# The samples' context in four column groups of TensorE, and a sample's final scores on VectorE in two turns

## The reference: what is computed

```python
def one_seq(args):                       # once for each of 8 samples
    qn_i, qr_i, pages, rows_i = args
    past = cache[pages].reshape(-1, CACHE_ROW)          # 2048 x 320
    rows = jnp.concatenate([past, rows_i], 0)           # + the sample's own row
    lat_i, kr_i = rows[:, :KV_LORA_RANK], rows[:, KV_LORA_RANK:]
    kn_i = key_nope(lat_i, w_uk, g_kn_nope)             # per head, rms-normalised
    return mla_attend(qn_i, qr_i, kn_i, kr_i, lat_i, ...)

# in mla_attend: s = scores of 8 heads x 2049 rows
p = jax.nn.softmax(s, axis=-1)
ctx = jnp.einsum('bhqk,bkc->bqhc', p, lat)              # 8 heads x 256
```

## Time and profile before

| | us |
|---|---|
| median of 3 runs | 3432.31 |
| lowest, highest | 3425.12, 3432.45 |
| the profiled execution's own time | 3436.75 |
| its span, first to last instruction | 3434.9 |
| TensorE busy | 2767.9 (81%) |
| VectorE busy | 2275.0 (66%) |
| ScalarE busy | 1041.1 (30%) |
| GpSimd busy | 1223.9 (36%) |
| mean granted TensorE clock | 0.887 |
| moved by DMA | 1264.74 MB |

### The profile page before, as it was taken

One profiled execution on the slowest core, in us unless ns is written; L12 is line 12 of the kernel. 1 busy time (PEld: TensorE's weight loads), 2 busy tenths in 40 slices (PEclk: granted clock), 3 DMA queues, 4 the chain that ended last, 5 costly groups with the idle time before them and its releaser, 6 DMA issues.

```text
span 3434.9 us, 39503 instructions
## 1 busy us (share of the span) xinstructions
PE 2767.9 (81%) x11255; PEld 1236.3 (36%) x11255; DVE 2275.0 (66%) x6378; ACT 1041.1 (30%) x4438; POOL 1223.9 (36%) x1077
## 2 busy tenths in 40 slices
PE   7898889979989878989988779889875675566766
PEld 2355554424434333434433244344331231112321
DVE  2444568887777876768776676777766545565455
ACT  1222324424334423434434314434311111111111
POOL 0000014434333434434434434433344444543343
PEclk8989999979999989989989989999988777777777
DMA  8740069999999999999999999999999999999998
GB/s 337 276 177 35 14 252 410 400 365 405 364 379 411 414 373 413 413 388 418 409 393 409 400 392 409 415 403 417 392 410 413 408 421 408 422 394 378 419 420 352
DMA packets 201396, 1264.74 MB, mean 368 GB/s; under 512 B 23689, under 2 KB 44730, under 8 KB 61393
## 3 DMA queue, kind: packets, MB, share of 16 engines
q0 software_dynamic: 150784, 1091.03, 77.8%
q1 hardware_dynamic: 50393, 171.18, 13.0%
HBM read 1258.79 MB, written 3.79 MB: 368 GB/s over the span
## 4 chain that ended last, share of the span: by engine, by line
PE 44%; DMA 29%; DVE 13%; issue 7%; ACT 3%; POOL 3%; SPq 0%; DVEq 0%; POOLq 0%; ACTq 0%; PEldq 0%
PE bank L1149 15%; DMA ring<-in_uv,work 14%; PE bank L887 7%; DMA big<-in_uv,work 7%; DMA mod_mix<-in_uv,work 6%; PE bank L999 5%; DVE ring L2031 2%; PE bank L833 2%; PE bank L904 2%; PE bank L701 2%; ACT work L1478 1%; DMA ring<-in_w_ada 1%; POOL ring L1517 1%; PE bank L639 1%; PE bank L731 1%
## 5 line engine op out<-in xcount | busy, mean ns | idle before, releaser
L1149 PE MATMUL bank<-ring,work 128*64 128x512 f32 (+1 forms) x2080 | 900.8, 706 | 243.7 <-ACT work L1478 243.7
L1517 POOL DMA_INDIRECT ring<-in_uv,work x520 | 609.8, 1173 | 906.2 <-PE bank L1149 781.1
L2031 DVE CUSTOM_DVE_ANT_0 ring<-ring,mod_smp 128x1024 f32<-128x1024 f32 x512 | 622.2, 1223 | 270.3 <-DMA ring<-in_uv,work 262.9
L1466 ACT ACTIVATE work<-work 128x2 f32<-128x2 f32 x520 | 105.1, 202 | 1478.2 <-DVE work L2031 1477.9
L1517 POOL DMA_INDIRECT big<-in_uv,work x260 | 309.0, 1189 | 670.8 <-PE bank L1149 369.5
L887 PE MATMUL bank<-big 128*128 128x512 f32 x1024 | 513.9, 625 | 0.0
L1149 PE MATMUL bank<-big,work 128*64 128x512 f32 (+1 forms) x1040 | 311.1, 716 | 157.9 <-ACT work L1478 157.9
L1149 PEld LDWEIGHTS bank<-ring,work 128*64 128x64 f32 (+1 forms) x2080 | 210.1, 153 | 593.4 <-ACT work L1478 356.7
L2031 DVE CUSTOM_DVE_ANT_0 big<-big,mod_smp 128x1024 f32<-128x1024 f32 x256 | 309.7, 1223 | 138.4 <-DMA big<-in_uv,work 134.6
L1149 PE MATMUL bank<-work 128*64 128x512 f32 (+1 forms) x520 | 292.9, 691 | 107.9 <-ACT work L1478 107.9
L1478 ACT ACTIVATE work<-small,work 128x64 f32<-128x64 f32 (+1 forms) x1040 | 303.2, 339 | 144.8 <-DVE work L2041 138.4
(11 more groups left out here) (301 smaller groups left out, 3422.5 us busy)
## 6 DMA issues: line engine op xcount, KB each, us to landing
big<-in_wk SPq DMA_DIRECT2D x48, 1152.0 KB, 10.4
ring<-in_w_ada SPq DMA_DIRECT2D x64, 768.0 KB
work<-in_cache_mla SPq DMA_DIRECT2D x104, 160.0 KB, 7.2
ring<-in_uv,work POOLq DMA_INDIRECT x520, 12.3
big<-in_uv,work POOLq DMA_INDIRECT x260, 12.2
ring<-in_w_mla_out SPq DMA_DIRECT2D x1, 4096.0 KB, 14.1
big<-in_w_mla_out SPq DMA_DIRECT2D x4, 1024.0 KB, 11.5
mod_smp<-in_cache_mla SPq DMA_DIRECT2D x24, 160.0 KB, 10.9
```

Source lines behind the costliest of these rows:

```text
L1149: last = mm(out, diag[:, t % 2, j, 0:min(m, HALF)], s[:, D + half * 512:D + (half + 1) * 512], start=(k == 0 and (n < S0 or j == 0)), stop ...
L1466: act.activation(acts[:, t % 2 * GRP:(t % 2 + 1) * GRP], dots[:, t % 2 * GRP:(t % 2 + 1) * GRP], ACT.Gelu)\
L1517: pool.indirect_dma_start(slot[g % SLOTS], None, T["uv"].rearrange("l e d -> (l e) d"), bass.IndirectOffsetOnAxis(index[:, k * GRP + j:k * ...
L2031: dve.tensor_tensor_reduce(u, u, hb, 1.0, 0.0, ALU.mult, ALU.add, dots[:, at:at + 1]).then_inc(sem("dots_set"), 1)
```

## The change

`tail` is given 8 turns instead of 7. `final_scores` stops after two of the three Newton steps, and a new `final_scores_end` does the rest in the next turn; everything behind it moves by one turn, `load_pages` on SP too. `context` writes block g to the column group g modulo 4 (output rows 0, 32, 64, 96). The first four blocks take 32 columns of `ps_all` as weights, so that all 32 rows of a group are written, of which 8 count; the rest take 8 columns. The four partial sums are not added there: `contexts` copies all 128 rows, unscaled, and `context_cols` multiplies each half with two slices of `fold` (ones where row modulo 64 equals the column), which transposes and adds in one. The division by the sum of the numerators moves behind it, into `keep_context`, for which `context` now spreads the sums to all 128 rows.

With it `tail` is at turns 34, 81, 121, 172, 215, 259, 302 and 345, and the samples' first pages at 2, 46, 89, 129, 180, 223, 270 and 310. The last page of sample 5 moves from turn 252 to 257.

```diff
@@ -243,7 +243,8 @@
         krn = region(big, NPG * NH, 16384)
         krt = region(big, NPG * NH, 16384)
         sc_s = region(big, (NPG + 1) * NH, 16384).rearrange("p (g h) -> p g h", g=NPG + 1)
-        ps_s = region(big, (NPG + 1) * NH, 16384).rearrange("p (g h) -> p g h", g=NPG + 1)
+        ps_all = region(big, (NPG + 1) * NH, 16384)
+        ps_s = ps_all.rearrange("p (g h) -> p g h", g=NPG + 1)
         ctx_s = region(big, KLC * NH * NS, 16384).rearrange("p (c h s) -> p c h s", c=KLC, h=NH)
         oT_s = region(big, NH * NS, 16384)
         pages = region(big, NS * NPG, 16384)[0:1].bitcast(I32)
@@ -339,8 +340,8 @@
                 page_turn[t_] = (r_, g_)
                 t_ += 2
             tail[r_] = t_
-            t_ += 7
-        out_turn = max(tail[NS - 1] + 7, head_turn(3, PH - 1) + 1)
+            t_ += 8
+        out_turn = max(tail[NS - 1] + 8, head_turn(3, PH - 1) + 1)
         assert out_turn + 10 < smp_open[S0], out_turn
 
         page_at = {page_turn[k]: k for k in page_turn}
@@ -528,7 +529,7 @@
                                 sp.wait_ge(sem("mix_w_free"), 3)
                             load_head(layer_of(n), i, h)
                 for r in range(1, NS):
-                    if t == tail[r - 1] + 4:
+                    if t == tail[r - 1] + 5:
                         sp.wait_ge(sem("ctx_ps"), r)
                         load_pages(r)
                 if t == AHEAD:
@@ -898,17 +899,21 @@
 
             def context(r):
                 pe.wait_ge(sem("p_sum"), r + 1)
-                mm(pb[6][0:NH, 144:145], tiny[:, 24:24 + NH], ones[:, 0:1], start=True, stop=True)
+                mm(pb[6][:, 144:144 + NH], ones[:, :], tiny[:, 24:24 + NH], start=True, stop=True)
                 pe.wait_ge(sem(f"page_in{NPG // PGRP}"), 16 * (r + 1))
                 for g in range(NPG + 1):
-                    last = mm(pb[6][0:NH, 160:160 + KL], ps_s[:, g, :], cached[g][:, 0:KL] if g < NPG else cached_own, start=(g == 0), stop=(g == NPG))
+                    at, m = g % 4 * 32, 32 if g < 4 else NH
+                    last = mm(pb[6][at:at + m, 160:160 + KL], ps_all[:, g * NH:g * NH + m], cached[g][:, 0:KL] if g < NPG else cached_own,
+                              start=(g < 4), stop=(g > NPG - 4), skip_group_check=True)
                 last.then_inc(sem("ctx_ps"), 1)
 
             def context_cols(r):
                 pe.wait_ge(sem("ctx_norm"), r + 1)
                 pe.sem_inc(sem("wait_done"), 1)
                 for c in range(KLC):
-                    last = pe.transpose(pb[6][:, 432 + c * NH:432 + (c + 1) * NH], ctx_n[c][0:NH, :], ident[0:NH, 0:NH])
+                    for a in range(2):
+                        last = mm(pb[6][:, 432 + c * NH:432 + (c + 1) * NH], ctx_n[c], fold[:, a * 32:a * 32 + NH],
+                                  start=(a == 0), stop=(a == 1), skip_group_check=True)
                 last.then_inc(sem("ctx_cols"), 1)
 
             def sample_heads():
@@ -1103,13 +1108,13 @@
                 if t in page_turn:
                     project_page(*page_turn[t])
                 for r in range(NS):
-                    if t == tail[r] + 1:
+                    if t == tail[r] + 2:
                         spread_max(r)
-                    if t == tail[r] + 2:
+                    if t == tail[r] + 3:
                         spread_max2(r)
-                    if t == tail[r] + 4:
+                    if t == tail[r] + 5:
                         context(r)
-                    if t == tail[r] + 6:
+                    if t == tail[r] + 7:
                         context_cols(r)
                 if t == out_turn:
                     sample_heads()
@@ -1533,10 +1538,11 @@
             d(tt(cact[:, :, 0:NC], hbuf[:, 0, 0:DC * NC].rearrange("p (c n) -> p c n", c=DC),
                  hbuf[:, 1, 0:DC * NC].rearrange("p (c n) -> p c n", c=DC), ALU.mult), "c_act")
 
-            def inverse_root(y, v, t, link):
-
-                link(ts(y.bitcast(I32), v.bitcast(I32), -0.5, float(0x5F3759DF), ALU.mult, ALU.add))
-                for _ in range(3):
+            def inverse_root(y, v, t, link, steps=(0, 1, 2)):
+
+                for step_ in steps:
+                    if step_ == 0:
+                        link(ts(y.bitcast(I32), v.bitcast(I32), -0.5, float(0x5F3759DF), ALU.mult, ALU.add))
                     link(tt(t, y, y, ALU.mult))
                     link(stt(t, t, -0.5, v, ALU.mult, ALU.mult))
                     link(stt(y, t, 1.5, y, ALU.add, ALU.mult))
@@ -1867,7 +1873,12 @@
                     w.next("own_in", 16)
                 e, at = chain(r, 0)
                 e(ts(kss[:, :], kss[:, :], 1.0 / NOPE, EPS, ALU.mult, ALU.add))
-                inverse_root(krn[:, :], kss[:, :], krt[:, :], e)
+                inverse_root(krn[:, :], kss[:, :], krt[:, :], e, (0, 1))
+
+            def final_scores_end(r):
+
+                e, at = chain(r, 8)
+                inverse_root(krn[:, :], kss[:, :], krt[:, :], e, (2,))
                 both = pb[6][:, 0:256].rearrange("p (g a h) -> p g a h", g=NPG, a=2)
                 e(tt(sc_s[:, 0:NPG, :], both[:, :, 0, :], krn[:, :].rearrange("p (g h) -> p g h", g=NPG), ALU.mult))
                 e(tt(sc_s[:, 0:NPG, :], sc_s[:, 0:NPG, :], both[:, :, 1, :], ALU.add))
@@ -1892,16 +1903,16 @@
 
             def contexts(r):
                 dve.wait_ge(sem("ctx_ps"), r + 1)
-                dve.reciprocal(tiny[0:NH, 32:33], pb[6][0:NH, 144:145]).then_inc(sem("smp_tail"), 1)
-                dve.wait_ge(sem("smp_tail"), r * 2 + 2)
+                dve.reciprocal(tiny[:, 24:24 + NH], pb[6][:, 144:144 + NH]).then_inc(sem("smp_tail"), 1)
                 for c in range(KLC):
-                    last = ts(ctx_n[c][0:NH, :], pb[6][0:NH, 160 + c * P:160 + (c + 1) * P], tiny[0:NH, 32:33], None, ALU.mult)
+                    last = ts(ctx_n[c], pb[6][:, 160 + c * P:160 + (c + 1) * P], 1.0, None, ALU.mult)
                 last.then_inc(sem("ctx_norm"), 1)
 
             def keep_context(r):
                 dve.wait_ge(sem("ctx_cols"), r + 1)
-                ts(ctx_s[:, :, :, r:r + 1].rearrange("p c h s -> p c (h s)"), pb[6][:, 432:432 + 2 * NH].rearrange("p (c h) -> p c h", c=KLC),
-                   1.0, None, ALU.mult).then_inc(sem("ctx_ready"), 1)
+                dve.wait_ge(sem("smp_tail"), r * 2 + 2)
+                tt(ctx_s[:, :, :, r:r + 1].rearrange("p c h s -> p c (h s)"), pb[6][:, 432:432 + 2 * NH].rearrange("p (c h) -> p c h", c=KLC),
+                   tiny[:, 24:24 + NH].unsqueeze(1).to_broadcast([P, KLC, NH]), ALU.mult).then_inc(sem("ctx_ready"), 1)
 
             def add_sample():
                 dve.wait_ge(sem("smp_out_ps"), 5)
@@ -1995,14 +2006,16 @@
                     if t == tail[r]:
                         final_scores(r)
                     if t == tail[r] + 1:
+                        final_scores_end(r)
+                    if t == tail[r] + 2:
                         top(r)
-                    if t == tail[r] + 2:
+                    if t == tail[r] + 3:
                         shift(r)
-                    if t == tail[r] + 3:
+                    if t == tail[r] + 4:
                         sums(r)
-                    if t == tail[r] + 5:
+                    if t == tail[r] + 6:
                         contexts(r)
-                    if t == tail[r] + 6:
+                    if t == tail[r] + 7:
                         keep_context(r)
                 if t == out_turn + 9:
                     add_sample()
```

## The result

| | us |
|---|---|
| before, median of 5 runs | 3432.45 |
| changed, median of 5 runs | 3450.32 (3446.35 to 3458.30) |
| ratio, with its 95% interval | 1.0051 (1.0038 to 1.0064) |
| changed, measured once more, median of 11 runs | 3445.99, ratio 1.0030 (1.0018 to 1.0042) |
| profiled execution of the changed kernel | 3446.35, span 3444.5 |

The change makes the kernel slower, by 0.3 to 0.5%. The forecast was 3421 us, and the time lies outside its range as well.

The account below looks back on a forecast made before the run. The DMAs were taken to bound the kernel, so only their dry time could return: -9 us (context), -2 (final_scores split), 0 (longer tail), in all -11 from 3432.3 to 3421 us; likeliest 3415 to 3427, 8 in 10 3407 to 3438.

Parts of the forecast that it names:

- What bounds: In the stage of the turns the DMAs set the pace; an engine counts only where the DMAs run dry.
- dry time: A window's length times one less its DMA share; 9.1 us at the tails' starts, 11.7 us from context on.
- Part 1, size: Context in column groups on TensorE: 2.2 us instead of 7.5 per sample, 9 us of kernel time given back.
- Part 1, the page load: TensorE's wait for the next sample's pages: about 2 of 7.00 us remain; 1 to 2 us new for sample 2.
- Part 3, sample 5: Sample 5's tail moves into the pooling mixer's turns: 0, between a gain of 2.5 us and a loss of 4.7.
- Part 2: final_scores in two turns on VectorE: 2.25 us move one turn on, 2 us gained, between 0 and 4.5.
- first windows: Four turns from each sample's tail (final_scores); samples 0 and 7 were to keep a DMA share of 0.90 to 0.95.
- rival (b): Windows from context on: bytes are right, the DMA share hides thin queues; up to 26 us back, 3406 us, chance 0.10.
- (d): Slower: less dense TensorE work in the tail keeps its clock low; some +8 us, 3440 us, chance 0.12.
- the windows from context on: Four turns from each sample's context; the granted clock there was to stay above 0.9.
- 0.97 or more in all windows: Sign that the forecast holds: a DMA share of at least 0.97 in every window from context on.

Follow-up runs that it names:

- second profile: The changed kernel measured once more without an edit, and profiled again: 3445.99 us, ratio 1.0030 to the kernel before.
- the padded kernel: The changed kernel with 24 useless TensorE instructions behind the context, after the signal that releases the page loads: 3439.16 us, ratio 1.0016 to the kernel before.
- the groups alone: The kernel before with only the context in four column groups, tail of 7 turns and final_scores in one: 3428.13 us, ratio 0.9985.

## Why the prediction was wrong, point by point

- **What bounds.** Right in the main. The largest losses appear as dry time of the DMAs; the busy time of TensorE fell by 27.5 us and bought nothing by itself. But turns 270 to 302 are 4 to 5 us longer than before at a share of 1.01, which dry time doesn't explain and no run here does.
- **Part 1, size.** Right: 2.3 us for 2.2 forecast, full overlap. By itself it gained 5 us where 9 were taken.
- **Part 1, the page load: the first step that failed.** I had written that of the 7.00 us wait "about 2 us of that remain", and took 1 to 2 us for sample 2 (the prediction names a load by the sample whose tail it ends, so these are the pages of sample 3, in turn 128). Measured were 13.3 us in the one place (turn 222 now) and 10.6 in the other. I had moved the release 5.3 us forward and kept the time to landing as it was. But that time was short before because TensorE, 7.5 us in its context, freed no slots, and the gathers' queue ran down: to 0.4 to 1.3 MB at the first issue for samples 2, 3, 5 and 7, against 1.5 to 3.3 MB in the changed kernel. POOL in turn 86 of the kernel before:

```profile
1005.42 0.94 POOL L1517 DMA_INDIRECT work<-in_uv,work  x1 [10.38 <-PE bank L1149]
```

  The shorter context removed the pause in which the pages had the DMAs nearly to themselves. What TensorE's stand costs is seen best in turns 220 to 232, between kernels with the same turns: the changed kernel (a stand of 13.27 us, and 79.5 us of length in its second profile), and the padded one (1.80 us).

```profile
1751.12:1831.77 80.65, 64.96 (x286) 31.32 (x284) 47.66 (x149) 26.23 (x127) 29.56 (x26) 0.87 0.94 365
```

```profile
1749.97:1824.07 74.10, 66.51 (x304) 31.70 (x303) 48.20 (x149) 26.27 (x126) 27.97 (x24) 0.95 1.01 403
```

  That is 5 to 7 us for this one stand, although the padded kernel has 5.34 us more work in these turns. Behind samples 1 and 6, with stands as long, the same comparison gives 1 us or nothing (turns 81 to 95: 86.9 and 85.8; 302 to 317: 84.5 and 85.2).

- **Part 3, sample 5: the second step that failed, and the larger one.** I had the move in the right place, and set it to 0 between a gain of 2.5 and a loss of 4.7 us, from VectorE's busy time alone. Measured: turns 254 to 270 went from 103.1 to 110.7 us (106.7 in the second profile), and dry time between turns 257 and 267 from 4.1 to 17.4 us (13.0). The 32 turns behind add 4 to 5 us. VectorE's busy time in turns 254 to 270 is the same before and after (79.7 and 79.6 us), so a sum of busy times could not show this; what I had left out is how a tail's steps and the mixer's hold each other up when they share turns. One part of it is seen: VectorE's stand for `spread_max` behind 7.5 us of matmuls, 6.68 us where it was 4.50. Taking that wait away gave nothing that can be measured. How the rest divides between the tail's steps and the page that now lies in these turns stays open.
- **Part 2.** Right in the main: nothing to gain where VectorE is full. The first windows of samples 0 and 7 went from 0.83 and 0.91 to 0.86 and 0.93. In sample 5's crowded turns the split did help, which I hadn't said; the time shows it clearly only against the second measurement of the changed kernel.
- **Rivals.** The slower side was named, 12%, but with the wrong mechanism. (The sum of rival (b) is short of its own words: 26 us and part 2's 4.5 give 3402, not 3406.) The clock did fall in the windows from context on (0.76 and 0.76 for samples 1 and 2, from 1.00 and 0.99), as (d) said. But TensorE stands for pages in just these windows, so the clock is as much a result as a cause. With the groups alone, where the stand in turn 87 is 2.0 us, turns 86 to 90 have a clock of 0.93, and that kernel is faster. Two windows, those of samples 1 and 2 (here from tail + 5 to tail + 9, in answer to the earlier trace rows):

```profile
990.54:1025.85 35.31, 21.93 (x129) 10.84 (x127) 19.80 (x63) 9.04 (x30) 9.02 (x9) 0.76 0.99 372
1225.60:1253.90 28.30, 16.57 (x77) 6.96 (x71) 15.99 (x33) 5.67 (x24) 7.45 (x7) 0.76 1.02 405
```

  The dry time in these two is gone, as forecast, but they are 8.7 and 3.5 us longer than those of the earlier trace rows (a turn later, with TensorE's stand for the pages inside). For samples 4 and 5 the share fell, from 0.96 and 0.97 to 0.92 and 0.87, so the sign "0.97 or more in all windows" was missed.

## What to carry to other kernels

When a step gets shorter on an engine that frees buffers, ask which transfers its length kept out of the way: a small urgent load that was quick beside an idle queue is slow beside a full one, and wants to be asked for earlier, here by a turn or two. When a schedule is counted in turns, look at every item that a longer period pushes across a boundary, and look at what else stands in the turns where it lands: busy times that add up to less than the turn don't say that it fits. Profile the changed kernel twice before a window's difference of a few us is believed. The gain of a faster step can be real and still be lost to its neighbours; measured alone, and with one turn more between the samples, this one is worth 0.27%.

## What the runs showed of the hardware that I had not expected

- Four column groups with only 8 columns each run side by side like groups of 32: 0.21 us per step of four for 256 columns in f32.
- Packets of two queues were taken nearly one for one while both had work: 511 of 1280 bytes beside 508 and 514 of 8192 bytes. Four loads of 160 KB in rows of 1280 bytes then landed 12 us after the fourth issue, and 2.0 to 2.5 us after it where at most 1.3 MB of gathers was left and none was issued (samples 2 and 7 of the kernel before).
- The changed kernel gave 1.0051 in one set of runs and 1.0030 in another, with intervals that just overlap. Differences of 0.2% between sets were read with that in mind.
